# Seven-product weight sums with other signs: the first by an adding transfer, the third from the second

## What is computed

```python
def hybrid_layer(x, positions, norm_mix, w_in, conv_w, w_conv_out, ret_norm, w_ret_out, w_o,
                 norm_mlp, w_up, w_down):
    h = rmsnorm(x, norm_mix)
    proj = h @ w_in
    cb, cc, cu, q, k, v, g, ga, gb = jnp.split(proj, split_points, axis=-1)
    y_conv = short_conv_mixer(cb, cc, cu, conv_w, w_conv_out)
    y_ret = retention_mixer(q, k, v, g, positions, ret_norm, w_ret_out)
    merged = jax.nn.sigmoid(ga) * y_conv + jax.nn.sigmoid(gb) * y_ret
    x = x + merged @ w_o
    h2 = rmsnorm(x, norm_mlp)
    return x + jnp.square(jax.nn.relu(h2 @ w_up)) @ w_down
```

## Time and profile before

| | us |
|---|---|
| median of 3 runs | 2099.52 (2098.48 to 2100.42) |
| span of the traced execution | 2097.1 |
| TensorE busy | 2074.6 |
| vector engine busy | 1564.8 |
| ScalarE busy | 1067.8 |
| POOL busy | 27.3 |

### The profile page before, as it was taken

The page is one execution under the profiler, slowest core; times in us unless marked ns, Lnnn a source line. Parts: engine busy times, 40 slices in busy tenths (PEclk is TensorE's granted clock), DMA queues, the critical chain, the costliest instruction groups (busy, mean ns, idle before and its releaser), DMA issues.

```text
span 2097.1 us, 30779 instructions
## 1 busy us (share of the span) xinstructions
PE 2074.6 (99%) x12382; PEld 1869.8 (89%) x12382; DVE 1564.8 (75%) x2113; ACT 1067.8 (51%) x1522; POOL 27.3 (1%) x36
## 2 busy tenths in 40 slices
PE   9999999999999999999999999999999999999998
PEld 8888878878888899988999998888899988999997
DVE  8787785768656778866878887756778866868884
ACT  5776474646434445524555654434445534555653
POOL 0000000000000000000000000000000000000000
PEclk9999999999999999999999999999999999999999
DMA  5332222212322234432434353322234432344352
GB/s 186 111 101 100 91 81 71 91 66 84 107 85 87 81 111 136 146 111 91 121 107 118 118 162 105 107 91 81 91 101 141 145 107 91 121 115 118 114 175 83
DMA packets 63870, 227.96 MB, mean 109 GB/s; under 512 B 7216, under 2 KB 7600, under 8 KB 63600
## 3 DMA queue, kind: packets, MB, share of 16 engines
q1 hardware_dynamic: 59040, 208.83, 29.8%
q0 software_dynamic: 4544, 17.04, 4.7%
q10 hardware_dynamic: 144, 0.12, 0.0%
HBM read 223.86 MB, written 2.10 MB: 108 GB/s over the span
## 4 chain that ended last, share of the span: by engine, by line
PE 83%; DVE 3%; ACT 1%; issue 1%; DVEq 0%; ACTq 0%
PE bank L846 15%; PE bank L848 15%; PE bank L847 15%; PE bank L891 9%; PE bank L895 9%; PE bank L893 9%; PE bank L841 2%; PE bank L842 2%; PE bank L843 2%; PE bank L1100 1%; PE bank L1092 1%; ACT arena L1676 0%; PE bank L1169 0%; PE bank L1170 0%; PE bank L1168 0%
## 5 line engine op out<-in xcount | busy, mean ns | idle before, releaser
L1894 DVE TENSOR_TENSOR w_lo<-w_raw,w_hi 128x1024 fp32r<-128x1024 f32 x477 | 572.3, 1216 | 370.9 <-ACT w_hi L1271 368.9
L1271 ACT ACTIVATE w_hi<-w_raw 128x1024 fp32r<-128x1024 f32 x477 | 490.9, 1047 | 513.8 <-PE bank L848 333.1
L846 PE MATMUL bank<-h_both,w_hi 128*128 128x512 f32 x956 | 365.2, 382 | 2.0 <-DVE arena L1940 1.1
L847 PE MATMUL bank<-h_both,w_hi 128*128 128x512 f32 x956 | 362.3, 379 | 0.0
L848 PE MATMUL bank<-h_both,w_lo 128*128 128x512 f32 x956 | 362.3, 379 | 0.0
L846 PE MATMUL bank<-y_hi,w_hi 128*128 128x512 f32 x920 | 351.1, 382 | 5.4 <-DVE y_lo L1945 3.4
L848 PE MATMUL bank<-y_hi,w_lo 128*128 128x512 f32 x920 | 349.4, 380 | 0.0
L847 PE MATMUL bank<-y_lo,w_hi 128*128 128x512 f32 x920 | 349.2, 380 | 0.0
L846 PEld LDWEIGHTS bank<-h_both,w_hi 128*128 128x128 f32 x956 | 180.7, 189 | 30.1 <-issue 3.5
L847 PEld LDWEIGHTS bank<-h_both,w_hi 128*128 128x128 f32 x956 | 180.7, 189 | 25.9 <-issue 1.0
L848 PEld LDWEIGHTS bank<-h_both,w_lo 128*128 128x128 f32 x956 | 180.7, 189 | 25.6
(11 more groups left out here) (340 smaller groups left out, 3624.9 us busy)
## 6 DMA issues: line engine op xcount, KB each, us to landing
w_raw<-in_stream SPq DMA_DIRECT2D x389, 512.0 KB, 3.6
w_raw<-in_stream POOLq DMA_DIRECT2D x30, 512.0 KB, 5.4
x<-in_x_t SPq DMA_DIRECT2D x8, 256.0 KB, 6.7
out_t<-x SPq DMA_DIRECT2D x8, 256.0 KB, 2.1
arena<-in_consts POOLq DMA_DIRECT2D x1, 1024.0 KB, 5.2
w_raw<-in_stream SPq DMA_DIRECT2D x2, 256.0 KB, 4.3
arena<-in_positions POOLq DMA_DIRECT2D x1, 256.0 KB, 6.0
vec_t<-in_vecs ACTq DMA_DIRECT2D x1, 112.5 KB, 3.2
```

What stands on the lines that cost most here:

```text
L846: pe.matmul(out, w_hi[:, slot, w], streamed(a_h), start=first, stop=False)
L847: pe.matmul(out, w_hi[:, slot, w], streamed(a_l), start=False, stop=False)
L1271: A.activation(w_hi[:, slot, w], w_raw[:, chunks.raw_slot[raw], w], ACT.Copy).then_inc(hi_ready, 1)
L1894: V.tensor_tensor(w_lo[:, slot, w], src[:, w], w_hi[:, slot, w].bitcast(F32), ALU.subtract).then_inc(lo_ready, 1)
```

## The change

The two quarters of the upper half change places in the stream: the first chunk is now B12, the second B11. The signs of T1, T2 and T3 change so that each weight sum but one is an addition:

- T1 = B12 + B11: an adding DMA from POOL's queue puts the second chunk of the stream onto the first slot, as soon as that slot's own load is in (semaphore `first_in`). The second chunk is also loaded as before, for B11 and T3.
- T2 = T1 + B22 in the first slot, by the vector engine behind T1's remainder.
- T3 = T2 - B11 in the second slot, by the vector engine, ahead of T2's remainder.
- T4 = T2 + B21 as before, by the adding DMA.

The signs of two activation sums, of two copies of `keep` (an activation Copy with scale -1) and of two sums in `y_mix` follow; one of these is a scalar_tensor_tensor where a tensor_tensor stood. TensorE's instructions stay as they are.

```diff
@@ Chunks
+            self.first_sums.append((slots[0], self.raw_loads[first], first + 1))
             self.fourth_sums.append((done + T2 + 1, slots[0], first + 3))
@@ POOL
-            for third_done, slot, c in chunks.fourth_sums:
-                pool.wait_ge(lo_ready, third_done)
-                pool.dma_start(w_raw[:, slot, :], stream[c, :, :], accum_op=ALU.add).then_inc(fourth_in, 16)
+            for (slot, loads, first_c), (second_done, _, last_c) in zip(chunks.first_sums, chunks.fourth_sums):
+                pool.wait_ge(raw_loaded[slot], 16 * loads)
+                pool.dma_start(w_raw[:, slot, :], stream[first_c, :, :], accum_op=ALU.add).then_inc(first_in, 16)
+                pool.wait_ge(lo_ready, second_done)
+                pool.dma_start(w_raw[:, slot, :], stream[last_c, :, :], accum_op=ALU.add).then_inc(fourth_in, 16)
@@ raw_of
-            at = {None: 0, B11: 0, T1: 0, T2: 0, B21: 3, T3: 1, B22: 2, T4: 0}[place]
-            if place == T4:
-                return raw + at, (fourth_in, 16 * (group + 1))
-            made = {T1: 1, T3: 2, T2: 3}.get(place)
-            return raw + at, made and (combined, 3 * group + made)
+            at = {None: 0, B11: 1, T1: 0, T2: 0, B21: 3, T3: 1, B22: 2, T4: 0}[place]
+            if place in (T1, T4):
+                return raw + at, (first_in if place == T1 else fourth_in, 16 * (group + 1))
+            made = {T2: 1, T3: 2}.get(place)
+            return raw + at, made and (combined, 2 * group + made)
@@ keep, for two of its four copies
-                    A.activation(out, src, ACT.Copy).then_inc(seeded, 1)
+                    A.activation(out, src, ACT.Copy, scale=sign).then_inc(seeded, 1)
@@ remainder
-                if place == T1:
-                    loaded(2)
-                    dve.wait_ge(combined, 3 * group + 1)
-                    V.tensor_tensor(raw[1], raw[2], raw[1], ALU.subtract).then_inc(combined, 1)
+                if place == T2:
+                    dve.wait_ge(combined, 2 * group + 1)
+                    V.tensor_tensor(raw[1], raw[0], raw[1], ALU.subtract).then_inc(combined, 1)
                 w = slice(0, used_columns(T, n))
-                src = raw[{B21: 3, T3: 1, B22: 2}.get(place, 0)]
+                src = raw[{B11: 1, B21: 3, T3: 1, B22: 2}.get(place, 0)]
                 dve.wait_ge(hi_ready, T.value("chunk", n + 1))
                 V.tensor_tensor(w_lo[:, slot, w], src[:, w], w_hi[:, slot, w].bitcast(F32),
                                 ALU.subtract).then_inc(lo_ready, 1)
-                if place == B11:
-                    loaded(1)
+                if place == T1:
+                    loaded(2)
                     dve.wait_ge(lo_ready, T.value("chunk", n + 1))
-                    V.tensor_tensor(raw[0], raw[1], raw[0], ALU.subtract).then_inc(combined, 1)
-                elif place == T1:
-                    dve.wait_ge(lo_ready, T.value("chunk", n + 1))
-                    V.tensor_tensor(raw[0], raw[0], raw[2], ALU.subtract).then_inc(combined, 1)
+                    V.tensor_tensor(raw[0], raw[0], raw[2], ALU.add).then_inc(combined, 1)
@@ y_mix
-                V.tensor_tensor(y_sum(0), y_sum(0), late, ALU.add).then_inc(summed, 1)
-                V.tensor_tensor(y_sum(1), y_sum(2), late, ALU.subtract).then_inc(summed, 1)
+                V.tensor_tensor(y_sum(0), y_sum(0), late, ALU.subtract).then_inc(summed, 1)
+                V.scalar_tensor_tensor(out=y_sum(1), in0=y_sum(2), scalar=-1.0, in1=late, op0=ALU.mult,
+                                       op1=ALU.subtract).then_inc(summed, 1)
@@ quarters
-        return np.stack([w[k, :, :, n].transpose(1, 0, 2).reshape(P, CW) for k, n in ((0, 0), (0, 1), (1, 1), (1, 0))])
+        return np.stack([w[k, :, :, n].transpose(1, 0, 2).reshape(P, CW) for k, n in ((0, 1), (0, 0), (1, 1), (1, 0))])
```

More of the change, by code:

```diff
@@ L334, in __init__ @@
         self.raw_slot, self.raw_loads, self.raw_free = [], [], []
-        self.fourth_sums = []
+        self.first_sums, self.fourth_sums = [], []
         free, loads = [0] * RING, [0] * RING
@@ L655, in build @@
         vecs_in = sem("vecs_in")
+        first_in = sem("first_in")
         fourth_in = sem("fourth_in")
@@ L1303, in ahead, with keep @@
                     round_ahead(n, (T.fixed["chunk"] + n) % RING)
-                def keep(out, src):
-                    A.activation(out, src, ACT.Copy).then_inc(seeded, 1)
+                def keep(out, src, sign=1.0):
+                    A.activation(out, src, ACT.Copy, scale=sign).then_inc(seeded, 1)
                 def mixed_highs():
@@ L1340, in seven @@
                     products(3)
-                    keep(last, sum_)
+                    keep(last, sum_, -1.0)
                     ahead(5)
@@ L1347, in seven @@
                     products(5)
-                    keep(kept(T, step, 1), sum_)
+                    keep(kept(T, step, 1), sum_, -1.0)
                     pay(1)
@@ L2615, in sums_of @@
                 for k in range(DT // 2):
-                    far, op = {0: (4, ALU.add), 1: (0, ALU.subtract), 2: (0, ALU.subtract), 3: (4, ALU.add)}[n]
+                    far, op = {0: (4, ALU.subtract), 1: (0, ALU.subtract), 2: (0, ALU.subtract), 3: (4, ALU.add)}[n]
                     t = slice(SEQ // 2, SEQ) if n == 0 else slice(0, SEQ // 2)
@@ L2623, in sums_of @@
                     V.scalar_tensor_tensor(out=mixed_k(step, n, k), in0=x[:, far + k, t], scalar=gain_column(step, far + k),
-                                           in1=added, op0=ALU.mult, op1=op).then_inc(summed, 1)
+                                           in1=added, op0=ALU.mult, op1=op, reverse1=n < 2).then_inc(summed, 1)
             def mixed_low(step, n, sums, highs):
```

## The result

The changed kernel has a median of 2133.14 us (2132.28 to 2135.07, 4 runs) against 2099.65 us of the kernel before, a ratio of 1.0161 with a 95% interval of 1.0147 to 1.0176. That is 33.5 us more. I had predicted 2103.0 us with a range up to 2111.0, so the time lies outside it. I had forecast a loss of 3.4 us. Even the largest of my cases, which had a chance of 0.20 and was worked out to +22.6 at its full price, fell short of the measured loss.

A forecast was written before the change was run, and what follows sets the result against it. TensorE, busy for 99% of the span, was taken to bound the kernel. Terms of -0.9 + 2.4 + 1.6 + 0.3 = +3.4 us gave 2103.0 us against the median of 2099.52, range 2098.4 to 2111.

The forecast's parts named there:

- What bounds the kernel, and what the removed work is worth: Seven-product groups: TensorE bounds; 36.8 us of removed vector work is hidden behind it, worth only -0.9 us.
- The 0.22 us gaps: TensorE's waits for B21, once in each of four seven-product down projections; claimed to close, -0.9 us.
- The signs at nothing: New activation signs and the scalar_tensor_tensor: same sizes as before, hidden by TensorE, costed at nothing.
- T3's place: Subtraction ahead of T2's remainder: T1's to T2's remainder 5.6 us instead of 4.44; 3.6 at the group at 1241.15.
- the four groups: Groups behind seven-product down projections (1142, 1219, 1927, 2004 us): T2 waits 0.6 us in each, +2.4 us.
- The landing of the first sum: POOL's adding transfer that makes T1 was to land 5.4 to 6.6 us after its issue.
- The rival in which transfer and loads share the engines: First sum lands up to 3.1 us later, 8.5 us: 2122 us, about 2110 at half that delay; chance 0.20.
- The worth of that landing: Waits from the chain slot, load, sum, T1, T2: +2.4 us in four groups, +1.6 and +0.3 in the next.
- The fourth sum beside the next group's first load: At the group at 1241.15 the load took 6.1 us beside an adding transfer; T2 waits, +1.6 us.
- B11 on the second load: B11's slot is free 1.2 us later; ScalarE's rounding and copy still fit: nothing, unless the load takes longer.
- cu and ga: Groups of ga behind cc and cu: 15.8 us of room where the chain takes 11.7, so no wait.
- The first rival: All sums are early enough and only the gaps close: 2098.6 us; chance 0.22.

The follow-up runs named there:

- early_groups_only: Kernel before with new signs and T3 from T2; T1 by adding transfer only in the twelve groups behind ordinary chunks, elsewhere by the vector engine; 2098.40 us (0.9993).
- b11_first: Changed kernel with T1 made by the vector engine and B11 the first chunk again; signs and T3's place stay; 2099.09 us (0.9998).
- short_third_fourth: Changed kernel with the loads of each group's third and fourth chunk cut to 64 of 1024 columns; 2111.99 us (1.0058).
- short_fourth_sum: Changed kernel with the fourth sum's transfer adding 64 of 1024 columns; 2122.14 us (1.0107).
- t1_by_vector: Changed kernel with T1 made by the vector engine behind B11's remainder instead of by transfer; 2111.39 us (1.0053).
- short_first_sum: Changed kernel with the first sum's transfer adding 64 of 1024 columns; 2102.93 us (1.0015).
- b11_first_by_transfer: Changed kernel with B11 the first chunk again and all thirty first sums by transfer onto the second load; 2164.03 us (1.0312).
- plain_first_transfer: Changed kernel with the first sum's transfer copying B11 over the slot instead of adding it; 2116.20 us (1.0074).

## Why the prediction was wrong, step by step

- **What bounds the kernel, and what the removed work is worth: right.** 38.0 us of vector work went without a gain. The 0.22 us gaps do close, in the changed kernel as in early_groups_only, and the latter shows that this is all there was: 1.1 us measured at most, 0.9 predicted. That nothing comes of the groups behind ordinary chunks was right too, by the same run.
- **The signs at nothing: right**, by b11_first (0.9998).
- **T3's place: right in the four groups, too small in the next ones.** Behind the down projections I had priced it (5.6 us from T1 to T2 instead of 4.4), and 5.6 came. In the groups behind these I had left 3.6 us, as if the subtraction ran while ScalarE rounds. The vector engine had only 0.5 us free there, and it takes 4.3 us now (1256.65 to 1260.95; vector engine, then TensorE):

```profile
1255.43 1.22 DVE L1897 TENSOR_TENSOR w_lo<-w_raw,w_hi 128x1024 fp32r<-128x1024 f32 x1 [4.07 <-ACT w_hi L1275]
1256.76 1.23 DVE L1902 TENSOR_TENSOR w_raw<-w_raw 128x1024 f32<-128x1024 f32 x1
1257.90 0.78 DVE L2745 TENSOR_TENSOR arena<-kept_t 128x512 f32<-128x512 f32 x1
1258.57 1.24 DVE L1893 TENSOR_TENSOR w_raw<-w_raw 128x1024 f32<-128x1024 f32 x1
1259.71 1.24 DVE L1897 TENSOR_TENSOR w_lo<-w_raw,w_hi 128x1024 fp32r<-128x1024 f32 x1
```

```profile
1256.71 0.38 PE L895 MATMUL bank<-mixed,w_hi 128*128 128x256 f32 x1 [0.38 <-DVE w_lo L1897]
1261.01 0.38 PE L895 MATMUL bank<-mixed,w_hi 128*128 128x256 f32 x1 [1.35 <-DVE w_lo L1897]
```

- **The landing of the first sum: wrong, the step that failed.** "5.4 us, at 1218.1 with 6.6" was taken from the fourth sums, which leave about one product (2.2 to 5.1 us) ahead of the next load. The first sum leaves among the loads, with B11's often still in flight: 7.5 us in the median, up to 9.4. I had written that no row shows an adding transfer with two loads behind it, and then took 6.6 us as the upper bound all the same. The rival in which transfer and loads share the engines was the one that came, with a chance of 0.20. Its full delay of 3.1 us gives a landing of 8.5 us and a time of 2122; the median landing stayed under that and the time went over it, so the landing is not all of the error. My evidence against it, 197 GB/s at 1228.5, was one half microsecond with one load beside the sum. The Trainium skill ("DMA: Bandwidth & Descriptors", "Queues, rings and completion order") says that each engine takes turns between its queues, packet by packet. This case's traces agree as far as the engines are shared: the landing falls from 7.5 to 5.5 us when both loads shrink. That the turns go packet by packet no run here shows.
- **The worth of that landing: the chain after it was right, its reach not.** In the group worked out, slot to issue (3.7 us) and T1 to T2 (5.6 us) came as predicted. But with the median landing that I had assumed, short_third_fourth still lost some 12 us where I had +3.4. In its trace the waits before T2 in the four groups are 0.3 to 0.7 us in three, near my 0.6, and 0.1 in the first; those in the next groups are 0.6 to 1.1 us in all four, where I had 0.1 in three (the 4.3 us above are 0.7 of each); and ScalarE's copies add 2.8 us.
- **The fourth sum beside the next group's first load: priced in one group only.** I had counted it in the group at 1241.15 (6.1 us for the load) and in no other that follows a group. short_fourth_sum puts 11 us on the size of these transfers. How much of a late T2 is handed on from group to group stays open.
- **B11 on the second load: wrong at nothing.** I asked only whether ScalarE's copy would still fit. t1_by_vector against b11_first gives 12.3 us when T1 is made behind B11. In the changed kernel T1 doesn't depend on B11's remainder, and little of this is left. Of its four waits for ScalarE's copies (3.2 us), two (0.36 us at 1164.58, 0.53 at 1250.73) are what I had named: the copy stands behind B11's rounding, which waited for its load (ScalarE in the changed kernel):

```profile
1249.05 1.06 ACT L1275 ACTIVATE w_hi<-w_raw 128x1024 fp32r<-128x1024 f32 x1 [2.77 <-DMA w_raw<-in_stream]
1250.01 0.58 ACT L1310 ACTIVATE kept_t<-bank 128x512 f32<-128x512 f32 x1
```

- **The other two copies: not in the prediction.** They are 1.15 us each, at 1189.23 and 1994.83, and no load stands ahead of them. ScalarE ran late there: it had waited for the vector engine to square the up projection's results (line 2780), which stands behind T2's remainder, and T1 and T2 had been made late. The same two waits are in short_first_sum, where they are 2.3 of the 3.3 us, and in b11_first_by_transfer, where B11 is the first chunk again, so they aren't B11's (ScalarE and TensorE in the changed kernel, then TensorE in b11_first_by_transfer):

```profile
1178.01 1.24 ACT L1481 ACTIVATE y_hi<-arena 128x512 fp32r<-128x512 f32 x2 [1.16 <-DVE arena L2780]
```

```profile
1189.23 0.35 PE L895 MATMUL bank<-h_both,w_hi 128*128 128x256 f32 x1 [1.15 <-ACT kept_t L1310]
```

```profile
1200.45 0.35 PE L895 MATMUL bank<-h_both,w_hi 128*128 128x256 f32 x1 [1.15 <-ACT kept_t L1310]
```

Even a sum of 64 columns came late ahead of them: in short_first_sum one was issued at 1156.34 and ScalarE waited for it until 1161.52.

- **cu and ga: wrong at nothing.** I compared 15.8 us of room with the chain to T1, 11.7. With a landing of 7.7 us in one ga group and 8.9 in the other, and 5.6 us from T1 to T2 there too, operands of ga were late, once in each layer: T2 by 2.3 us at 869.1, and T1 and T2 by 1.2 and 2.9 us at 1667 and 1673 (the trace's 2.13, 0.99 and 2.69, each with the 0.17 us explained under the sum of the loss).
- **Small things in the prediction.** The first rival's time is 2098.6 in its own line and 2098.4 in the range; nothing hangs on it.
- **The sum of the loss.** The waits in the groups are 26.2 us; the rest of the 36.2 us by which the span grew is, as an estimate, restart and clock. A wait costs some 0.27 us more than the trace's figure for it. At 1239.21 that figure, 2.23 us, counts from the end of the matmul before (1236.71 + 0.28), but without the wait the next would have begun 0.11 behind its start, 0.17 earlier; and the second behind the wait stands at double spacing, 0.22 instead of 0.11. Nineteen waits (15 + 4) make 5 us. The last 5 are the clock, below: 26.2 + 5 + 5 = 36.2.

## What to carry to other kernels

A transfer that is cheap where it runs nearly alone is not cheap among others: take its landing from a row that has the same neighbours, and where there is none, let the bound grow by the whole engine time of what will run beside it, what is already in flight included (here 5.4 + 3 x 1.6 = 10.2 us, with 9.4 measured at the longest). An operand that needs two transfers in series has its slack cut by both, and by whatever slows the first of them. A late operand also delays what stands behind it on the other engines (here a copy 17 us later), so a chain of groups has to be worked through one after the other, not once and times four. Work taken from an engine that idles 25% of the time behind a full TensorE is worth only the gaps that it causes, and these can be counted beforehand.

## What the runs showed of the hardware

An adding transfer takes twice the time of the DMA engines that a plain one takes, with the same bytes from HBM: 3.07 against 1.58 us for 512 KB (on POOL's queue itself 1.5 us less for each plain one), and 7.5 against 5.1 us to its landing in the same place (changed kernel against plain_first_transfer), of which some 0.3 us are the shorter issue.

TensorE's clock fell to its lower level at some of the new waits. Behind the wait of 2.1 us in the trace that ended at 869.1 the granted clock was 0.50, that is 1.2 GHz, then half of each, and at 874 it was back at 2.4 GHz (1.00). The last row is of the wait that ended at 1958.95, in which it fell before the wait was over:

```profile
865.00:870.00 5.00, 2.87 (x24) 2.68 (x23) 4.93 (x7) 3.44 (x4) 0.66 (x1) 0.96 0.00 0
870.00:872.00 2.00, 2.00 (x11) 2.00 (x10) 2.00 (x3) 0.60 (x1) 0.20 (x1) 0.50 0.66 74
872.00:874.00 2.00, 2.00 (x15) 2.00 (x15) 1.26 (x2) 0.29 (x1) 0.00 (x0) 0.74 0.99 197
874.00:876.00 2.00, 2.00 (x21) 2.00 (x20) 0.71 (x1) 2.00 (x3) 0.00 (x0) 1.00 0.91 320
...
1957.00:1958.90 1.90, 0.00 (x0) 0.00 (x0) 1.90 (x3) 1.55 (x2) 0.00 (x0) 0.89 0.00 0
```

It happened at three waits (869, 1172, 1959 us; 2.1 to 2.7 us), and not at two others as long (2.2 us at 1239 and 2.7 at 1673). Some 47 matmuls stand 0.1 us too far apart in these stretches, about 5 us of the loss in all. Why it fell at three of the five stays open.
